# The token factor of block one's norms behind the first products, with the first loads and the lower bounds moved

## The reference

```python
def rms_norm(x, g):
    xf = x.astype(jnp.float32)
    y = xf * lax.rsqrt(jnp.mean(xf * xf, axis=-1, keepdims=True) + EPS)
    return (y * g.astype(jnp.float32)).astype(x.dtype)
...
    for l in range(DEPTH):
        h = rms_norm(x, norm_mix[l])
        z = h @ w_in[l]
        (q_a, k_a, v_a, q_h, i_h, f_fw, f_bw, g_h, a_c, g_c) = jnp.split(z, splits, axis=-1)
...
        x = x + mix @ w_out[l]
        h = rms_norm(x, norm_mlp[l])
        x = x + jnp.square(jax.nn.relu(h @ w_mlp_in[l])) @ w_mlp_out[l]
```

## Time and profile before

| | us |
|---|---|
| median of 3 runs | 3778.51 |
| lowest, highest | 3776.96, 3781.1 |
| the profiled execution | 3782.67 |
| its span | 3780.9 |
| PE busy | 3603.8 (95%) |
| DVE busy | 2106.8 (56%) |
| ACT busy | 1398.6 (37%) |
| POOL busy | 869.3 (23%) |

### The profile page before, as it was taken

How to read it: one execution, slowest core, us unless ns; L and a number is a source line. 1 busy time by engine, 2 the same in 40 slices (tenths; PEclk the granted TensorE clock), 3 DMA queues, 4 the chain that set the end, 5 groups by cost and what they waited for, 6 DMA issues and landing times.

```text
span 3780.9 us, 47130 instructions
## 1 busy us (share of the span) xinstructions
PE 3603.8 (95%) x18583; PEld 2904.8 (77%) x18583; DVE 2106.8 (56%) x2762; ACT 1398.6 (37%) x1873; POOL 869.3 (23%) x716
## 2 busy tenths in 40 slices
PE   7989999998999999999899999999989999989998
PEld 5667888766788878887567888788868778777887
DVE  5967444596743454347666444633574655665434
ACT  4664332366432332223663212222233434332223
POOL 3210655321065536552213640000000000000000
PEclk9999999999999999999899999999999999999999
DMA  6212655421265556663224643233322222223331
GB/s 162 64 44 67 152 142 143 106 75 44 66 154 138 150 117 150 146 153 70 61 68 101 161 127 91 81 98 100 101 76 76 73 76 87 63 66 89 100 90 67
DMA packets 564437, 377.56 MB, mean 100 GB/s; under 512 B 37489, under 2 KB 561354, under 8 KB 564218
## 3 DMA queue, kind: packets, MB, share of 16 engines
q1 hardware_dynamic: 564218, 374.56, 37.6%
HBM read 372.32 MB, written 2.17 MB: 99 GB/s over the span
## 4 chain that ended last, share of the span: by engine, by line
PE 77%; DVE 16%; ACT 4%; issue 2%; SPq 0%; DMA 0%; DVEq 0%; ACTq 0%
PE bank L446 62%; DVE conv_sum L1290 2%; PE bank L454 2%; DVE w_lo L424 2%; PE bank L492 2%; PE bank L893 1%; PE bank L486 1%; ACT w_hi L415 1%; PE bank L487 1%; DVE std L955 1%; DVE norm_tmp L1749 1%; DVE norm_tmp L1743 1%; DVE X L1745 1%; DVE dil_probs L2542 1%; PE bank L2376 1%
## 5 line engine op out<-in xcount | busy, mean ns | idle before, releaser
L446 PE MATMUL bank<-H_hi,w_hi 128*128 128x512 f32 x2384 | 958.3, 402 | 5.4 <-DVE w_lo L424 1.8
L446 PE MATMUL bank<-H_hi,w_lo 128*128 128x512 f32 x2384 | 932.9, 391 | 0.0
L446 PE MATMUL bank<-H_lo,w_hi 128*128 128x512 f32 x2384 | 932.1, 391 | 0.0
L424 DVE TENSOR_TENSOR w_lo<-w_raw,w_hi 128x2048 fp32r<-128x2048 f32 (+3 forms) x285 | 654.6, 2297 | 147.7 <-ACT w_hi L415 139.5
L415 ACT ACTIVATE w_hi<-w_raw 128x2048 fp32r<-128x2048 f32 (+3 forms) x285 | 529.1, 1857 | 307.5 <-DMA w_raw<-in_ffn_w_up 129.3
L446 PEld LDWEIGHTS bank<-H_hi,w_hi 128*128 128x128 f32 x2384 | 448.8, 188 | 131.3 <-issue 38.4
L525 POOL TENSOR_TENSOR w_mod_raw<-w_mod_raw,silu_c 128x1024 f32<-128x1024 f32 x144 | 280.3, 1946 | 1169.5 <-DMA w_mod_raw<-in_w_mod 1123.6
L446 PE MATMUL bank<-U_hi,w_hi 128*128 128x512 f32 x1376 | 539.5, 392 | 3.8 <-DVE note L1012 3.8
L446 PE MATMUL bank<-U_hi,w_lo 128*128 128x512 f32 x1376 | 535.9, 389 | 0.0
L446 PE MATMUL bank<-U_lo,w_hi 128*128 128x512 f32 x1376 | 535.6, 389 | 0.0
L446 PEld LDWEIGHTS bank<-H_hi,w_lo 128*128 128x128 f32 x2384 | 448.7, 188 | 96.6 <-issue 0.3
(11 more groups left out here) (370 smaller groups left out, 4632.5 us busy)
## 6 DMA issues: line engine op xcount, KB each, us to landing
w_mod_raw<-in_w_mod SPq DMA_DIRECT2D x576, 128.0 KB, 5.8
w_raw<-in_ffn_w_gate SPq DMA_DIRECT2D x88, 512.0 KB, 4.0
w_raw<-in_ffn_w_up SPq DMA_DIRECT2D x88, 512.0 KB, 5.4
w_raw<-in_dil_w_in SPq DMA_DIRECT2D x36, 1024.0 KB, 5.1
w_raw<-in_w_mlp_in SPq DMA_DIRECT2D x32, 1024.0 KB, 6.0
w_raw<-in_w_mlp_out SPq DMA_DIRECT2D x32, 1024.0 KB, 5.8
w_raw<-in_ffn_w_down SPq DMA_DIRECT2D x32, 1024.0 KB, 5.4
w_raw<-in_w_in SPq DMA_DIRECT2D x16, 1024.0 KB, 5.6
```

The source lines that it names most:

```text
L424: dve.eng.tensor_tensor(WL[u % SLOTS][:, 0:n], RAW[u % SLOTS][:, 0:n], WH[u % SLOTS][:, 0:n].bitcast(F32), ALU.subtract).then_inc(lo_done. ...
L446: mm = pe.eng.matmul(bank[0:m, :], w[:, k, c0:c0 + m], r[:, k, :], start=(k == 0 and i == 0), stop=(k == kt - 1 and i == 2))
```

## The change

- In the two places of each layer with a norm, `pe_raw_pair` takes the place of `pe_pair`: the first two units run on X times gain alone (`raw_high` on ACT, `raw_low` on DVE). The sums, the warm-up and the spread of rstd stand between passes of this pair: behind pass 4 in up, behind passes 0 and 1 in layer 1's z0. In layer 0's z0 the pair is made one unit after the other, with the bias products behind pass 5 of the first, the sums behind its last and the spread behind the first pass of the second.
- Scaled halves of H are made meanwhile (`scaled_high`, `scaled_tiles`), each when the pair is done with the raw tile, for the units that follow; the third unit waits for them tile by tile. The four raw output tiles are multiplied by bank 5 afterwards, by DVE (`z_scaled`, `scale_mid`).
- In `last_mix` and `add_to_x` the raw halves are made tile by tile; `last_mix` makes the low halves of the weights first. w_hi and w_lo of the third unit are made ahead of the scaling.
- The first loads: SP issues the first two units of w_in right behind x; the parameter tables of the first half are issued by ACT, the rest by SP behind the first two units.
- silu(c) moves behind the heads' squares of layer 0; the lower bounds move to points 54 and 58 of the mixer.

The diff, cut:

```diff
+            units[lin[("z", l)][0]]["waits"] = "tiles"
...
-                add_units(("up", l, q), H, [square(w1, D_FF, 1024 * q + 256 * i) for i in range(4)], "none" if q else "tiles")
+                add_units(("up", l, q), H, [square(w1, D_FF, 1024 * q + 256 * i) for i in range(4)], "none")
+                if q == 0:
+                    units[lin[("up", l, q)][2]]["waits"] = "tiles"
...
+        def pe_raw_pair(pe, u, at_pass, apart=False):
...
+            sets = [todo[0:2], todo[2:4]] if apart else [todo]
+            for s, together in enumerate(sets):
+                pe.eng.wait_ge(lo_done.sem, u + (s + 1 if apart else 2))
+                for k in range(DT):
+                    if s == 0:
+                        pe.eng.wait_ge(raw_hi.sem, raw_hi.next(pe))
+                    for wh, wl, place, turn in together:
+                        if k == 0:
+                            pe.eng.wait_ge(acc_free[place].sem, turn - 1)
+                        pe.eng.matmul(banks[place][:], wh[:, k], rh[:, k, :], start=(k == 0), stop=False)
+                        pe.eng.matmul(banks[place][:], wl[:, k], rh[:, k, :], start=False, stop=False)
+                    if s == 0:
+                        pe.eng.wait_ge(raw_lo.sem, raw_lo.next(pe))
+                    for wh, wl, place, turn in together:
+                        mm = pe.eng.matmul(banks[place][:], wh[:, k], rl[:, k, :], start=False, stop=(k == DT - 1))
+                        if k == DT - 1:
+                            mm.then_inc(acc_ready.sem, acc_ready.add())
+                    if k < DT - 1 and s == len(sets) - 1:
+                        mm.then_inc(raw_used.sem, raw_used.add())
+                    for job in at_pass.get((s, k), ()):
+                        job(pe)
...
-        def keep_warm(pe, u, n):
+        def keep_warm(pe, u, n, beneath=False):
             place, turn = acc_place[units[u]["tiles_end"] - 4]
-            pe.eng.wait_ge(acc_free[place].sem, turn)
+            place = 5 if beneath else place
+            pe.eng.wait_ge(rbc_used.sem if beneath else acc_free[place].sem, rbc_used.taken["pe"] if beneath else turn)
...
+        def mixh_squares(act, l):
...
+            for t in range(4):
+                high(t)
+            square_of(0)
+            square_of(1)
+            for t in range(4, DT):
+                high(t)
+            split_hi(act, lin[("up", l, 0)][2])
+            for t in range(2, DT):
+                square_of(t)
...
+        def raw_high(act, t, gain):
+            act.eng.activation(H[0][:, t, :], X[:, t, :], ACT.Identity, scale=gain(t)).then_inc(raw_hi.sem, raw_hi.add())
+            act.eng.wait_ge(raw_hi.sem, raw_hi.made)
+
+        def raw_low(dve, t, gain):
+            dve.eng.wait_ge(raw_hi.sem, raw_hi.next(dve))
+            dve.eng.scalar_tensor_tensor(H[1][:, t, :], X[:, t, :], gain(t), H[0][:, t, :].bitcast(F32), ALU.mult, ALU.subtract).then_inc(raw_lo.sem, raw_lo.add())
+            dve.eng.wait_ge(raw_lo.sem, raw_lo.made)
+
+        def scaled_high(act, u, ahead_of):
+            for t in range(DT):
+                for job in ahead_of.get(t, ()):
+                    job()
+                act.eng.wait_ge(scaled.sem, scaled.next(act))
+                if t < DT - 1:
+                    act.eng.wait_ge(raw_used.sem, raw_used.next(act))
+                else:
+                    act.eng.wait_ge(acc_ready.sem, units[u + 1]["tiles_end"])
+                act.eng.activation(H[0][:, t, :], NT[2 + t % 2][:], ACT.Identity).then_inc(part_hi.sem, part_hi.add())
+                act.eng.wait_ge(part_hi.sem, part_hi.made)
+
+        def scaled_tiles(dve, gain, ahead_of):
+            ve = dve.eng
+            dve.eng.wait_ge(rbc_ready.sem, rbc_ready.next(dve))
+            for t in range(DT + 1):
+                if t < DT:
+                    ve.scalar_tensor_tensor(NT[2 + t % 2][:], X[:, t, :], gain(t), banks[5][:], ALU.mult, ALU.mult).then_inc(scaled.sem, scaled.add())
+                    dve.eng.wait_ge(scaled.sem, scaled.made)
+                for job in ahead_of.get(t, ()):
+                    job()
+                if t:
+                    dve.eng.wait_ge(part_hi.sem, part_hi.next(dve))
+                    ve.tensor_tensor(H[1][:, t - 1, :], NT[2 + (t - 1) % 2][:], H[0][:, t - 1, :].bitcast(F32), ALU.subtract).then_inc(rhs_ready.sem, rhs_ready.add())
+                    dve.eng.wait_ge(rhs_ready.sem, rhs_ready.made)
+
...
+                if gain and t:
+                    raw_low(dve, t - 1, gain)
+                if gain and t == DT - 1:
+                    raw_low(dve, t, gain)
...
         def last_mix(dve, l):
-            u = lin[("mixh", l)][0]
+            u, gain = lin[("mixh", l)][0], lambda t: colp("norm_mlp", 8 * l + t)
+            split_lo(dve, u + AHEAD)
             for t in range(DT):
                 bank, free = acc_take(dve, u, t)
                 dve.eng.tensor_tensor(X[:, t, :], X[:, t, :], bank[:], ALU.add).then_inc(free.sem, free.add())
                 dve.eng.wait_ge(free.sem, free.made)
-                if t >= 2:
-                    add_squares(dve, t - 1)
-            split_lo(dve, u + AHEAD)
+                if t in (4, 5):
+                    raw_low(dve, t - 4, gain)
+            for t in range(2, DT):
+                raw_low(dve, t, gain)
+                add_squares(dve, t - 1)
+            split_lo(dve, lin[("up", l, 0)][2])
+            rstd_column(dve)
...
+        def scale_mid(dve, u, j):
+            place, turn = acc_place[units[u]["tiles_at"] + j]
+            dve.eng.wait_ge(acc_free[place].sem, turn)
+            dve.eng.tensor_tensor(MID[j][:], MID[j][:], banks[5][:], ALU.mult).then_inc(high_scaled.sem, high_scaled.add())
...
+                if q == 0 and n == 1:
+                    for j in range(2):
+                        scale_mid(dve, u, j)
...
+            put(54, ("bound", 0))
+            put(58, ("bound", 1))
...
-            pe_pair(pe, lin[("z0", l)][0])
+            if l == 0:
+                jobs = {(0, 5): [bias_products], (0, DT - 1): [after_bias, pe_running_sums], (1, 0): [pe_spread]}
+            else:
+                jobs = {(0, 0): [pe_running_sums], (0, 1): [pe_spread]}
+            pe_raw_pair(pe, lin[("z0", l)][0], jobs, l == 0)
...
+        def z_scaled(dve, u, j, slot):
+            place, turn = acc_place[units[u]["tiles_at"] + j]
+            dve.eng.wait_ge(acc_free[place].sem, turn)
+            dve.eng.tensor_tensor(Z[:, slot, :], Z[:, slot, :], banks[5][:], ALU.mult).then_inc(high_scaled.sem, high_scaled.add())
...
+        def prologue_sp_tables(sp):
+            param_loads(sp, (2, 3))
+            sp.eng.dma_start(FIX[:, P:], io["fixed"][:, P:]).then_inc(fixed_in.sem, fixed_in.add(16))
...
+        def after_bias(pe):
+            pe.eng.wait_ge(bias_rows.sem, bias_rows.next(pe))
...
+            for t in range(2):
+                raw_high(act, t, lambda t: colp("norm_mix", t))
+            split_hi(act, 0)
+            for t in range(2, 4):
+                raw_high(act, t, lambda t: colp("norm_mix", t))
+                square_of(t - 2)
+            split_hi(act, 1)
+            for t in range(4, DT):
+                raw_high(act, t, lambda t: colp("norm_mix", t))
+                square_of(t - 2)
+            for t in range(DT - 2, DT):
+                square_of(t)
             sq_summed.taken["act"] += 1
 
-        def prologue_act_rest(act):
+        def modulation_act(act):
+            act.eng.wait_ge(rstd_ready.sem, 1)
+            act.eng.activation(CSIL[:], colp("c_2", 0, 32), ACT.Silu).then_inc(csil_ready.sem, csil_ready.add())
+            act.eng.wait_ge(csil_ready.sem, csil_ready.made)
...
                 if u == 2:
+                    prologue_sp_tables(sp)
                     prologue_sp_rope(sp)
...
-                norm_pe(pe, running=True, warm=lin[("z0", l)][0] - 1 if l else None)
-                if l == 0:
-                    pe.eng.wait_ge(bias_rows.sem, bias_rows.next(pe))
                 mixer_pe(pe, l)
                 hgrn_pe(pe, l)
                 pe_mixh(pe, l)
-                norm_pe(pe, running=True, warm=lin[("mixh", l)][0])
+                pe_raw_pair(pe, lin[("up", l, 0)][0], {(0, 4): [pe_running_sums, lambda w: keep_warm(w, lin[("mixh", l)][0], 3, True), pe_spread]})
                 for q in range(4):
-                    pe_linear(pe, ("up", l, q), q == 0)
+                    for u in lin[("up", l, q)][2 if q == 0 else 0:]:
+                        pe_unit(pe, u)
                     pe_linear(pe, ("down", l, q))
...
+                first = lin[("z0", l)][0]
+                act_std(act, D, True)
+                split_hi(act, first + 2)
+                copies = [lambda t=t: z_evac(act, first + t // 2, t % 2, t) for t in range(4)]
+                scaled_high(act, first, {0: copies[0:2]} if l == 0 else {DT - 1: copies[0:2]})
+                for copy in copies[2:4]:
+                    copy()
                 mixer_act(act, l)
                 hgrn_act(act, l)
```

(71 more changed lines are left out.)

124 lines of the change are left out of this document (79 added, 45 removed).

## The result

The changed kernel took 3785.44 us in the median (3780.58 to 3791.43, 20 runs), the kernel before beside it 3778.24 (20 runs). The ratio is 1.0021, with a 95% interval of 1.0014 to 1.0028: slower by 0.2%, where 3772.8 and a range of 3762 to 3782 had been forecast. The profiled run took 3785.45, its span was 3783.7.

The account below looks back on a forecast made before the run. TensorE's work plus its waiting gaps was taken as the bound. Norms -3.6, -2.7 and -2.0, start -2.5, POOL +2.5, lower bounds +2.6 sum to -5.7 us: median 3778.51 becomes 3772.8, range 3762 to 3782.

Parts of the forecast that it names:

- A: Start of the kernel, layer 0's first norm: first product near 21.0 in place of 31.68 us, POOL starting near 61.
- gain 2.5: At the start: the third unit's first z copy near 60.0 in place of 62.52 us, a gain of 2.5 us.
- POOL beside the rope: Layer 0's rope chain: POOL's later products hold back DVE's two-input instructions, 2.5 us lost out of 0 to 10.4.
- R3: Rival, chance 0.12: POOL and DVE shut each other out in the rope tiles, costing 17.4 us; total 3787.7 us.
- SP's queue: At the start: a weights' load waits behind POOL's first tile until about 66 us, which costs nothing.
- Lower bounds, 2.6: Layer 0's mixer, 118 to 200 us: the small DVE instructions moved there find little cover and cost 2.6 us.
- B: Layer 0's MLP norm: third unit 28.0 us after the stage before ends, in place of 32.9; net gain 3.6 us.
- C: Layer 1's mixer norm: third unit 26.5 us after the stage before ends, in place of 28.5; gain 2.0 us.
- D: Layer 1's MLP norm: third unit 28.0 us after the stage before ends, in place of 32.0; net gain 2.7 us.
- the wait of 1.3 for w_lo: First up stage of both MLP norms: TensorE waits 1.3 us for the fourth unit's low weights, behind DVE's added multiplications.
- R1: Rival, chance 0.23: multiplications, lower bounds and POOL's products all hide, so 13.4 us is kept; total 3765.1 us.
- R2: Rival, chance 0.15: at both MLP norms scaled tiles take 0.8 us more each, so nothing is gained there; total 3779.1 us.

Follow-up runs that it names:

- fill: The changed kernel with 20 matmuls whose result nobody uses, right behind layer 0's z0 pair; 3786.27 us, 1.0024 of the kernel before.
- silu_fill: The changed kernel with silu(c) back at the start and 20 unused matmuls behind the z0 pair; 3786.99 us, 1.0020 of the kernel before.

## Why the prediction was wrong

- *A, the times of the start: right.* First product 21.0 (20.96), POOL 61 (61.61).
- *A, "gain 2.5": the step that failed.* I let TensorE wait for the scaled tiles, counted the waits at their length, and took the gain at the first z copy (60.0, measured 61.56) for the gain of the stage. The waits were 1.27 and 0.55 us, but the clock fell to 0.50 at 56.0 and stayed there to 76.5 (a third wait, 0.26, came behind the fall), and the first rope product came 6.16 later in place of 2.5 sooner. I had priced the low clock at the first products only, where the trace of before shows it. fill shows that it is this: the scaled tiles at the same pace, no waits, clock 1.00 from 60 to 75, lag -0.53. Of the sum's other terms, the bias products, put at 2.6 without a row for their time at the full clock, took 2.10.
- *A, POOL beside the rope: 2.5, a quarter of the way.* With the clock as it was, 1.1 (6.16 to 7.28). But that is only because the chain came late: with the clock held, POOL costs 7.7 (fill). Each cause alone takes 6 to 7 us, both together no more. My R3 was this mechanism at 17.4: in fill eleven of the fifteen instructions ran over 0.69, by 8.1 us in all; in the kernel before six did, by 2.5. That it would hide behind another loss I did not see. My row of 2.43 was not of the chain, but of the convolution's product right behind it. The Trainium skill ("SBUF — State Buffer", "Who interferes with whom"), which lets the second of a two-input DVE instruction and a GpSimd instruction that reads SBUF wait for the whole of the first, agrees: 2.27 began behind a POOL instruction, 0.69 came where there was none (96.01 in fill) or where DVE began first (74.87). That all fifteen would be held, as its extreme, no run shows.
- *SP's queue: right.* No split of weights waited for its load.
- *Lower bounds, 2.6: right,* 2.9. The way was the exchange with ACT more than DVE's time. That the clock held behind the wait was luck of this profile: in five other profiles with the bounds in the mixer they cost 4.4 to 5.8.
- *B, C, D, the third unit: right.* T + 28.2, T + 26.1 and T + 28.0, where T + 28.0, 26.5 and 28.0 stood; C's wait for w_lo too (705.30 is T + 1.4; 1.3).
- *B and D, the wait of 1.3 for w_lo: mis-sized.* It is 2.9 in D. In B 1.7 went to a low clock behind the wait of 2.46, and 1.2 to w_lo, 2.9 together. DVE's U_lo took 1.67 in place of 0.69 beside POOL:

```profile
1041.21 1.36 POOL L565 TENSOR_TENSOR w_mod_raw<-w_mod_raw 128x512 f32<-128x512 f32 x1
...
1041.45 1.67 DVE L1012 TENSOR_TENSOR U_lo<-mid,U_hi 128x512 fp32r<-128x512 f32 x1
```

- *What the later norms are worth.* Counted 8.3; measured, by the medians, 1.4 with the waits for w_lo and 6.3 without most of them (intervals of 0.9988 to 1.0007 and 0.9975 to 0.9993). Besides the waits, part of what I took as the old gaps' length was low clock of the one profile I had.
- *R1* (covers hold) fell, as the rope and the bounds show; *R2* too: the scaled tiles came at their pace.

## What to carry to other kernels

A wait put into TensorE's stream costs its length and perhaps the clock behind it: look at what follows, and fill the wait or take it away. When two engines can each set the end of a stretch, taking one cost away shows nothing; take both before you call either innocent. And work that is taken out of a gap, small as it is, has to be placed where no exchange between engines hangs on it.

## What the runs showed of the hardware

The clock, once low at 56, stayed low for 20.5 us, though TensorE was busy without a gap from 59.8; in fill the same instructions ran at 1.00 up to the first rope product. Waits as short as 0.96 and 0.69 us stood ahead of a fall in silu_fill. The length of a wait alone did not tell: 2.46 in B was followed by a clock of 0.59 and 2.41 in D by 1.00; 2.79 at the lower bounds was followed by 1.00 in the changed kernel, and 2.80 to 2.86 by low clock in five other profiles. With 20 filling matmuls the clock held in fill and not in silu_fill, with 22 and 28 it held. A two-input DVE instruction of 0.69 us took up to 2.27 beside POOL's in fill. Two profiles of one kernel agree within 0.5 us for the first 200 us and differ by up to 6.2 behind, by where low clock fell.
